# The third mixer of a two-block transformer kernel, written as one pipeline of 23 steps

## The reference, cut to what matters

```python
def mla_heads(z, ...):
    cq, ckv, kr = z[..., :256], z[..., 256:384], z[..., 384:]
    q = (rmsnorm(cq, q_norm_g) @ w_uq)            # 8 heads x 96
    kv = (rmsnorm(ckv, kv_norm_g) @ w_ukv)        # 8 heads x (64 key + 64 value)
    k = concat(kv[..., :64], kr for every head)   # 96
    q, k = rmsnorm(q, qn_g), rmsnorm(k, kn_g)     # per head
    # latent tokens: rotary on the last 32 of q and of k
def attend(q, k, v):
    p = softmax((q @ k.T) * 96 ** -0.5); return p @ v
# retention, per head h, forward (with diagonal) and backward (without), as one masked product:
#   o = sum_j (q_i . k_j) * decay_h(i, j) * v_j,  latent scans start from the context's state
#   r = head_norm(o) * silu(rg)                   # mean and variance over 64
y = concat(a, r) @ w_out
mod = (silu(c) @ ada_w[l] + ada_b[l])             # 6 x 1024, for c and for c_ctx
```

## Time and profile before

| | us |
|---|---|
| median of three runs | 2829.38 |
| lowest and highest of them | 2822.4, 2833.46 |
| the profiled execution, whole time | 2824.94 |
| the profiled execution, span from first to last instruction | 2823.2 |
| part of the span from the end of `proj`'s last PE work to OutProj's first matmul | 305.6 |

### The profile page before, as it was taken

The page is one execution under the profiler, slowest core; times in us unless marked ns, Lnnn a source line. Parts: engine busy times, 40 slices in busy tenths (PEclk is TensorE's granted clock), DMA queues, the critical chain, the costliest instruction groups (busy, mean ns, idle before and its releaser), DMA issues.

```text
span 2823.2 us, 35104 instructions
## 1 busy us (share of the span) xinstructions
PE 2451.9 (87%) x14650; PEld 1887.0 (67%) x14650; DVE 1465.1 (52%) x2319; ACT 1049.6 (37%) x1752; POOL 199.5 (7%) x294
## 2 busy tenths in 40 slices
PE   5987688999997887878997987777999998989899
PEld 3834356888875666668995733235777877868899
DVE  5426545556546577755454143243656562881444
ACT  3234344222224445445444243243432233321543
POOL 0001100000000122210000011100110200000110
PEclk8998899999998999979998998878999999989999
DMA  6243271544433344324542131123244434334353
GB/s 252 82 180 147 95 268 47 164 142 133 163 114 90 120 147 152 136 81 146 180 151 103 44 119 42 67 100 149 92 147 150 148 112 165 123 126 164 120 179 135
DMA packets 172286, 372.25 MB, mean 132 GB/s; under 512 B 6848, under 2 KB 99264, under 8 KB 157920
## 3 DMA queue, kind: packets, MB, share of 16 engines
q1 hardware_dynamic: 172128, 370.01, 37.1%
HBM read 339.55 MB, written 30.44 MB: 131 GB/s over the span
## 4 chain that ended last, share of the span: by engine, by line
PE 71%; DVE 15%; ACT 7%; issue 2%; DMA 2%; POOL 1%; DVEq 0%; ACTq 0%; POOLq 0%
PE ps L169 70%; DVE sb_R L200 5%; ACT sb_R L248 2%; PE ps L179 1%; DVE sb_R L232 1%; DVE sb_WP L200 1%; DVE sb_H L200 1%; DVE sb_R L229 1%; DVE sb_X L217 1%; DVE sb_slot L200 1%; ACT sb_WP L254 1%; DVE sb_cst L200 1%; ACT L244 1%; DVE sb_cst L214 1%; ACT sb_slot L248 1%
## 5 line engine op out<-in xcount | busy, mean ns | idle before, releaser
L169 PE MATMUL ps<-sb_HP,sb_WP 128*128 128x512 f32 (+1 forms) x5568 | 1053.0, 351 | 61.7 <-DVE sb_WP L200 36.4
L169 PEld LDWEIGHTS ps<-sb_HP,sb_WP 128*128 128x128 f32 x5568 | 901.3, 195 | 191.7 <-issue 36.0
L200 DVE TENSOR_TENSOR sb_WP<-sb_slot,sb_WP 128x1024 fp32r<-128x1024 f32 x356 | 438.7, 1238 | 643.4 <-ACT sb_WP L254 643.3
L254 ACT ACTIVATE sb_WP<-sb_slot 128x1024 fp32r<-128x1024 f32 x356 | 374.1, 1057 | 788.6 <-PE ps L169 777.5
L169 PE MATMUL ps<-sb_XP,sb_WP 128*128 128x512 f32 (+1 forms) x2592 | 450.8, 336 | 10.2 <-DVE sb_XP L200 10.2
L169 PEld LDWEIGHTS ps<-sb_XP,sb_WP 128*128 128x128 f32 x2592 | 398.7, 190 | 62.4 <-DVE sb_XP L200 12.2
L200 POOL TENSOR_TENSOR sb_R<-sb_R 128x128 f32<-128x128 f32 (+2 forms) x194 | 146.3, 778 | 1962.5 <-ACT sb_R L248 1527.6
L169 PE MATMUL ps<-sb_R 128*32 128x64 f32 (+8 forms) x2088 | 198.7, 299 | 92.8 <-DVE sb_R L200 49.1
L169 PEld LDWEIGHTS ps<-sb_R 128*32 128x32 f32 (+5 forms) x2088 | 132.9, 156 | 169.1 <-issue 99.2
L200 DVE TENSOR_TENSOR sb_R<-sb_R 128x256 f32<-128x256 f32 (+3 forms) x398 | 194.5, 523 | 14.5 <-ACT sb_R L248 11.3
L248 ACT ACTIVATE sb_R<-ps 128x512 f32<-128x512 f32 (+1 forms) x208 | 99.4, 514 | 146.7 <-PE ps L169 143.2
(11 more groups left out here) (127 smaller groups left out, 2045.9 us busy)
## 6 DMA issues: line engine op xcount, KB each, us to landing
sb_slot<-mlp_w SPq DMA_DIRECT2D x32, 2048.0 KB, 9.0
sb_slot<-mod_w SPq DMA_DIRECT2D x22, 2048.0 KB, 7.7
sb_R<-ada_w SPq DMA_DIRECT2D x12, 2048.0 KB, 7.4
sb_slot<-ada_w SPq DMA_DIRECT2D x12, 2048.0 KB, 7.4
sb_slot<-ffn_w_gate SPq DMA_DIRECT2D x22, 1024.0 KB, 5.2
sb_slot<-ffn_w_up SPq DMA_DIRECT2D x22, 1024.0 KB, 7.7
sb_slot<-ffn_w_down SPq DMA_DIRECT2D x10, 2048.0 KB, 7.9
sb_slot<-odd_w_in SPq DMA_DIRECT2D x32, 512.0 KB, 7.2
```

The source lines that it names most:

```text
L169: return self.e.matmul(out, w, x, start=start, stop=stop, skip_group_check=True)
L200: return BLANK if self.e is None else self.e.tensor_tensor(out, a, b, op)
L254: return self.e.activation(out, a, ACT.Copy) if scale is None else self.e.activation(out, a, ACT.Copy, scale=scale)
```

## The change

The three threads become one loop, written out by hand on each engine: 23 steps (`steps` = 16 units + LAG 5 + 2). In step s the engines do

- item s of 16 (QH or KH of a head: make, copy, square, sum), and the rest of item s-1 (Ln, Exp, product, rotation); a head's tensors stand in a ring of four, so head h waits for the scores of the last unit that read head h-4 (`ring_free`);
- attention unit t = s-5: its scores, maximum, exponent and norm, all in one step; transposes and copies of unit t-1; values of unit t-2;
- retention: two rotations in each of steps 0 to 3; from step 4 one key block J of two heads at once (their score matmuls on rows 0 to 63 and 64 to 127, side by side in the queue, each to its own bank); every four steps the value products of two heads, in turns on columns 0 to 63 and 64 to 127 of one bank; then mean, variance and scaling in the three steps behind;
- the turn of the modulation: one, in the steps with attention two. `Mods` 3 now has 24 loads of 1 MB in two halves of slot 0 (`kn=1`), with four matmuls each, and no pause.

Score banks of attention stay 3 and 4, transposes 5, values 6; everything else takes banks 0 to 2 in turn. DJ has four pairs of tiles in place of one. The decay exponents F and R go to p.H. `w_out`'s first load waits for both halves of slot 0, the second for the last rotation and the last DJ. The count of matmuls, ACT functions and DVE products is the same, except that 12 groups of eight modulation matmuls are 24 of four.

```diff
 class Mods:
-    def __init__(self, p, n, W, bias, blk, l, pre, post, pre2, post2, pause, bufs, more_bufs=None):
+    def __init__(self, p, n, W, bias, blk, l, pre, post, pre2, post2, pause, bufs, more_bufs=None, kn=2):
...
-            for q in range(4):
-                view = self.view(4 * r + q)[1]
+            for q in range(self.nq):
+                view = self.view(self.nq * r + q)[1]
                 e.wait_ge("full", q)
-                for k in range(2):
+                for k in range(self.kn):
...
 class Mla:
+    LAG = 5
...
+    def PJ(self, hh, J):
+        at, n = 1536 * hh + (0, 512, 1024, 1280)[J], T if J < 2 else TC
+        return self.p.slots[3][:, at:at + n]
...
-        e.slot_until(self.su, ("mla.lat", ("made", 7, 1)))
-        for g in range(12):
+        e.slot_until(self.su, ("mla.lat", ("roped", (7, 1))), ("mla.ret", ("DJ", 7)))
+        e.slot_free(0)
+        for g in range(self.more.loads):
             self.more.load(sp, g)
+        e.slot_until(0, *[(self.more.name(2), ("rows", q)) for q in (6, 7)])
...
+    def make_act(self, e, n):
+        h, y = divmod(n, 2)
+        ps = e.wait_ge("made", h, y)
+        self.ring_free(e, h)
+        dst = self.KH[0:64, h % 4, :] if y else self.QH[0:96, h % 4, :]
+        e.copy(dst, ps[0:64 if y else 96, :]).then_inc(*e.sig("head", h, y))
+        e.wait_ge("head", h, y)
+        if y:
+            e.wait_ge("krope", h)
+        if n >= 2:
+            e.wait_ge("hsum", (h - 1, y))
+        self.items[n][0].square(e)
...
+    def blocks(self, s):
+        r = s - 4
+        at = lambda lag: (r - lag) // 4 if r >= lag and (r - lag) % 4 == 0 and (r - lag) // 4 < 4 else None
+        return divmod(r, 4) if 0 <= r < 16 else None, at(4), at(5), at(6)
+    def decays(self, s):
+        return {1: 0, 2: 1, 5: 2, 7: 3, 9: 4, 11: 5, 13: 6, 15: 7}.get(s)
...
     def pe(self, pe):
...
-        together(self.latent_pe(pe), self.retention_pe(pe), self.more.pe(pe))
+        e, r, A = pe.on("mla.lat"), pe.on("mla.ret"), self.attend
+        mods = self.more.pe(pe)
+        self.latents_pe(e)
+        for s in range(self.steps):
+            t, t1, t2, n, n1 = self.unit(s), self.unit(s - 1), self.unit(s - 2), self.item(s), self.item(s - 1)
+            if t1 is not None:
+                A.turn(e, t1, 0)
+            if t2 is not None:
+                A.values(e, t2)
+            if t1 is not None:
+                A.turn(e, t1, 1)
+            if t is not None:
+                e.wait_ge("roped", (2 * (t // 4) + 1, 1))
+                A.scores(e, t)
+            next(mods, None)
+            if n1 is not None:
+                self.rope_pe(e, n1)
+            if n is not None:
+                self.make_pe(e, n)
+            self.retention_pe(r, s)
+            if s in (3, 4):
+                self.values_pe(e, (2 * s - 6, 2 * s - 5))
+            if n is not None:
+                self.items[n][0].pe(e)
+            if t is not None:
+                next(mods, None)
+        at_once(mods)
...
     def act(self, act):
...
+        self.gates_act(r)
+        self.latents_act(e)
+        for s in range(self.steps):
+            t, t1, t2, n, n1 = self.unit(s), self.unit(s - 1), self.unit(s - 2), self.item(s), self.item(s - 1)
+            if n1 is not None:
+                self.root_act(e, n1)
+            if t1 is not None:
+                A.copies(e, t1)
...
+            if t2 is not None:
+                A.gather(e, t2)
+            if t is not None:
+                A.exps(e, t)
+            next(mods, None)
+            if n is not None:
+                self.make_act(e, n)
+            self.retention_act(r, s)
...
     def dve(self, dve):
...
+            if n is not None:
+                self.make_dve(e, n)
+            if n1 is not None:
+                self.items[n1][0].dve(e)
+            if t is not None:
+                A.maxima(e, t)
+            if n1 is not None:
+                self.rope_dve(e, n1)
+            if t is not None:
+                A.norms(e, t)
+            next(mods, None)
+            self.retention_dve(r, s)
...
-            Mods(p, 3, "ada_w_2", "ada_b", 1, 1, *second, 3, (slot(0),))]
+            Mods(p, 3, "ada_w_2", "ada_b", 1, 1, *second, 0, [(f"0{a}", p.slots[0][:, 2048 * i:2048 * i + 2048]) for i, a in enumerate("ab")], kn=1)]
```

544 lines of the change are left out of this document (272 added, 272 removed).

## The result

| | before | changed kernel |
|---|---|---|
| median (lowest to highest), us | 2826.09 (2822.4 to 2833.46) | 2731.68 (2730.53 to 2733.42) |
| ratio to before, 95% interval | | 0.9663 [0.964, 0.9687] |
| span of the profiled execution | 2823.2 | 2731.6 |
| stage: from `proj`'s last PE work to OutProj's first matmul | 306.25 | 209.66 |
| of it PE busy, PE not busy | 228.1, 78.2 | 171.8, 37.8 |

The change gained 94 us; the forecast was 70, and 2759 lies 27 us above the time, the low end of its range 3 us above it. The direction and the walk of a step hold; the two terms put on top of the walk, for the clock and for hand-overs, don't.

The account below looks back on a forecast made before the run. It took no engine as the stage's bound, but round trips between engines and a clock falling with PE's idle time. 211 us plus 15 for clock and 10 for hand-overs gave 236 against 305.6, hence 2759; range 2735 to 2795.

Parts of the forecast that it names:

- the walk of a step: In the loop, engine work followed from sum to sum at the upper clock: 10.6, 9.5, 9.8 and 9.65 us by kind.
- the clock: Over the stage's chain, some 135 us of PE work at granted clock 0.90 would take 15 us longer.
- hand-overs: In the loop, unseen waits on the three-bank ring: bounds 0 and 1 us a step, 10 us taken in all.
- latents: Ahead of step 0, the latents' norm stays at 6.9 us; the gates' table load was one paid a little later before.
- steps 0 to 4: Loop start without attention: step 0 takes 5 us; steps 1 to 4 take 30, at 6.7 or 8.5 each.
- steps 5 to 15: Middle of the loop: eleven steps, 108 us less 3, plus retention values and small jobs, 118 us.
- steps 16 to 22: End of the loop: each attention unit's own round is the chain, 47 us with retention values in two steps.
- the end: Behind the loop, before OutProj's first matmul: only three HP copies, one copy and one DVE product for WP, 4.3 us.
- Denser than that: Rival for the stage: short gaps keep the upper clock and the ring costs nothing; gain 90, 2739 us, chance 0.14.
- The ring's rival: In 16 item steps, sums also wait for DVE's norm and retention product, 32 us; gain 38, 2791 us, chance 0.18.
- Loads: Rival for modulation loads: halves don't overlap, a pair costs 15.4 us, 64 over 13 steps; gain 6, 2823, chance 0.03.
- The clock's fall: Rival for the loop: stops put the clock near 0.5, doubling 135 us of PE work; 2880 us, chance 0.04.

Follow-up runs that it names:

- less PE: Changed kernel with modulation matmuls of Mods 3 cut from 512 to 32 columns for 21 of 24 groups; 2731.84 us, stage 209.86.
- more ACT: Changed kernel with one more ACT exponent per attention unit, ahead of its own two, into an unused buffer; 2739.16 us, stage 215.48.
- whole loads: Changed kernel with modulation loads as before: 12 of 2 MB through one slot, eight matmuls each at every second turn; 2745.78 us, stage 224.20.
- short decays: Changed kernel with the decays' two exponents on 32 columns in place of 512 for every head but the first; 2728.91 us, stage 209.45.
- gates later: Changed kernel with the retention gates' small operations put behind the latents' norm on ACT and DVE; 2726.24 us, stage 206.73.
- weights early: Changed kernel with gates behind the latents' norm, and OutProj's first weight piece split within the last step; 2721.91 us, stage 204.45.

## Why the prediction was right in its direction and wrong in its size

In short: two terms put on top of the sum failed, 15 us for the clock and 10 us for hand-overs. The runs show the loop at 1.00 for 142 us and no wait for a bank of the ring. The sum at the upper clock, 211 us, came within 1.5 us of the stage, in part since its errors cancel (10 too long in the middle, 9 too short around it), which is luck; the walk of the steps is not, as shown below. The 25 us put on top of it didn't come. By its own terms:

| term | forecast | measured |
|---|---|---|
| latents | 6.9 | 10.0 |
| steps 0 to 4 | 5 + 30 | 34.3 |
| steps 5 to 15 | 118 | 108.0 |
| steps 16 to 22 | 47 | 50.1 |
| the end | 4.3 | 7.3 |
| clock | 15 | 0 from 1646.6 to 1788.9; the low rows of the latents and of steps 16 to 22 are in the 10.0 and the 50.1 |
| unseen hand-overs | 10 | none apart |
| sum | 236 | 209.7 |

*The clock, 15 us: the step that failed most.* It took 0.90, the granted clock of the head rows, for the whole chain, since PE was 94% busy there. But the 94% were busy time already stretched by the low level. In the changed kernel steps 5 to 15 have PE 90% busy (97.3 of 108) at 1.00. The busy share of a stretch at a mixed clock told nothing of a denser one. What the clock still cost can be estimated from rows that stand elsewhere at the upper level: 1.6 us in the latents (the first sum, below) and about 4 in steps 16 to 22, so 5 to 6 in place of 15. The claim "0.85 to 0.95" was wrong: 1.00 in the loop's first 142 us, 0.90 in its last 50, 0.96 in all. The forecast of PE's own work, 177 at the upper clock, was near (171.8 busy, at 0.96).

*Hand-overs, 10 us.* With two banks they come, and the stage is 31 us longer, the lower clock included; with three no wait of this kind is in PE's list. The bounds of 0 and 1 us a step held, and I had taken a middle where the lower one came.

*Steps 5 to 15, 10 us too long.* Forecast for the loop's kinds of steps, 9.5 to 10.6, the marks of the eleven steps are 6.4 (the first, which has no unit behind it), 8.9, 10.2, 12.4, 9.7, 10.0, 9.2, 12.8, 9.1, 10.0 and 9.3. The six plain steps of 9 to 15 sum to 57.3 where the walk said 57.9, and the two with values 25.2, forecast 26.2. The walk of a step was right, and it had PE's queue up to the make as the longer way (8.25) with DVE and ACT close behind (7.8); the experiments with less PE and more ACT find just these two ways, now one ahead, now the other. The 8.2 us added for head norm, decays and row copies were not on the path. Taking the decays away gave nothing, which shows it for them; for the row copies and the norm it is argued from the same sums. So "11.5 us a step" was 9.8.

*Latents and the end, 3 us too short each.* That the gates' table load was "one which was paid a little later" was the step that failed at the start. It now stands ahead of the squares, and PE's first sum waits 3.38 us for ACT where it waited 1.43; the sum itself then runs at the lower level, 3.58 in place of 1.95.

```profile
1640.02 3.58 PE L169 MATMUL ps<-sb_slot,sb_cst 128*128 128x512 f32 x4 [3.38 <-ACT sb_slot L248]
```

With the gates behind the norm again the wait is 1.43, the sum 1.96, and the latents give 2.2 us of the 3. At the end the sum had counted ACT's copies into HP and WP alone. What stands ahead of them, Ln, Exp and two products of the last head norm (1839.02 to 1841.8), is the other 3 us.

*Steps 16 to 22, 3 us short.* PE waits 3.93 us for DVE's norm there, and the rows behind it run at the lower level (the transposes at 1.12, in the earlier trace rows 0.66); PE in order of time:

```profile
1822.95 1.12 PE L179 MATMUL ps<-sb_cst,sb_R 128*128 128x128 f32 x4 [3.93 <-DVE sb_R L200]
1823.99 1.12 PE L169 MATMUL ps<-sb_slot,sb_R 128*64 128x128 f32 x8
```

*What held.* The waits for DVE's norm fell to 5.7 ("under 10"); no `ada_w` wait; a score pair in 1.13 ("about 1.0") and a values pair in 2.80 ("2.8"); the last modulation turn stands in step 17. The values' gain was less than 11: serial, a pair takes 4.57, not 5.6, so the four pairs saved 6 to 7. A single head's share of the 4.57 is 2.29. The 2.79 that I had doubled stands three times in the kernel before (1725.06, 1756.12, 1773.14), at the first of these places with a granted clock of 1.00; why two heads one after the other take less than twice that isn't shown.

*The rivals.* "Denser than that", 2739 at a chance of 0.14, came nearest, and for its two reasons. Of its "against", the gaps in steps 0 to 4 came and the clock stayed at 1.00; those in 16 to 22 did lower it, to 0.90. It should have had the larger chance: the row of 0.90 on which the forecast leaned was itself a row of the old order. The ring's rival, 32 us, has about the price of two banks (30.9), which is in part luck, as its wait for DVE's norm didn't grow and the clock did the rest; it doesn't hold for three. Loads never took the place. The clock's fall, the rival at 2880, didn't come here, but whole loads show its kind, at up to 14.5 us.

What stays open: why the same gap of 2.01 us in step 7 is crossed at the upper level in some kernels and not in others. The scores behind it take 1.88 in the changed kernel and in its second execution, with serial values, with more ACT in the unit and with the short decays; they take 3.62 with less PE, but also 2.53 with the gates later and 2.45 with the weights early, where PE has the very same work ahead of it in the loop. So less work ahead isn't the whole reason. And the start of the stage moves by 8 us between runs of like kernels, in the stages ahead; that wasn't looked into.
